# Encoder layer, attention stage: probability-value products 128 columns wide, scores over all 128 rows, the sink as a score column

## What is computed

```python
N_HEADS, N_KV_HEADS, HEAD_DIM, BLOCK = 8, 2, 64, 128        # GROUP = 4 query heads for each key/value head
scores = einsum('bnqkgd,bnskd->bnkgqs', qb, kb) * HEAD_DIM ** -0.5   # 128 queries against 3 * 128 keys
scores = scores - slopes * dist
scores = where(valid, scores, -1e30)
probs = softmax(concatenate([scores, sink_logit], -1), -1)[..., :-1]
out = einsum('bnkgqs,bnskd->bnqkgd', probs, vb)
```

## Time and profile before

| what | value |
|---|---|
| time, median of 3 runs | 3343.45 us (3343.38 to 3344.64) |
| profiled execution, its own time | 3344.08 us |
| span of the profiled execution | 3342.5 us |
| busy over the span: PE, DVE, ACT, POOL | 3062.5, 1164.3, 714.6, 487.1 us |
| mean granted clock of PE | 0.896 of full speed |
| attention part of the mixers | from about 803 us to about 1257 us of the span |

### The profile page before, as it was taken

One profiled execution on the slowest core, in us unless ns is written; L12 is line 12 of the kernel. 1 busy time (PEld: TensorE's weight loads), 2 busy tenths in 40 slices (PEclk: granted clock), 3 DMA queues, 4 the chain that ended last, 5 costly groups with the idle time before them and its releaser, 6 DMA issues. The chain is left out here.

```text
span 3342.5 us, 36601 instructions
## 1 busy us (share of the span) xinstructions
PE 3062.5 (92%) x13014; PEld 2447.1 (73%) x13014; DVE 1164.3 (35%) x1396; ACT 714.6 (21%) x1160; POOL 487.1 (15%) x829
## 2 busy tenths in 40 slices
PE   6699999838999997898894999999999997999998
PEld 5588888636666665687783788888888886788886
DVE  5000000167656550643333422222222222323432
ACT  4011111114333331500212311111111111212221
POOL 1530000164875000000111000000000000000111
PEclk9899999968555558899997999999999998999999
DMA  3322221241111005443544211111111113534553
GB/s 120 76 75 75 75 72 62 73 59 29 33 33 33 24 25 100 162 163 123 188 138 120 72 48 50 50 50 49 39 44 50 50 44 113 150 88 131 169 153 121
DMA packets 298294, 278.18 MB, mean 83 GB/s; under 512 B 46337, under 2 KB 269825, under 8 KB 288513
## 3 DMA queue, kind: packets, MB, share of 16 engines
q1 hardware_dynamic: 253536, 160.94, 17.2%
q0 software_dynamic: 13248, 68.16, 5.7%
q10 hardware_dynamic: 31456, 48.42, 4.7%
HBM read 191.50 MB, written 83.89 MB: 82 GB/s over the span
## 5 line engine op out<-in xcount | busy, mean ns | idle before, releaser
L325 PE MATMUL gu_banks<-gu_feat_hi,gu_w_hi 128*128 128x512 f32 (+1 forms) x1408 | 549.8, 391 | 1.0 <-DVE gu_feat_lo L235 1.0
L326 PE MATMUL gu_banks<-gu_feat_hi,gu_w_lo 128*128 128x512 f32 (+1 forms) x1408 | 548.4, 389 | 0.0
L327 PE MATMUL gu_banks<-gu_feat_lo,gu_w_hi 128*128 128x512 f32 (+1 forms) x1408 | 548.3, 389 | 0.0
L325 PE MATMUL pi_banks<-pi_feat_hi,pi_w_hi 128*128 128x512 f32 (+1 forms) x832 | 326.7, 393 | 31.0 <-DVE pi_w_lo L317 30.1
L327 PE MATMUL pi_banks<-pi_feat_lo,pi_w_hi 128*128 128x512 f32 (+1 forms) x832 | 324.9, 391 | 0.0
L326 PE MATMUL pi_banks<-pi_feat_hi,pi_w_lo 128*128 128x512 f32 (+1 forms) x832 | 324.9, 391 | 0.0
L325 PEld LDWEIGHTS gu_banks<-gu_feat_hi,gu_w_hi 128*128 128x128 f32 x1408 | 264.9, 188 | 55.9 <-DVE gu_feat_lo L235 1.4
L327 PEld LDWEIGHTS gu_banks<-gu_feat_lo,gu_w_hi 128*128 128x128 f32 x1408 | 264.7, 188 | 55.1
L326 PEld LDWEIGHTS gu_banks<-gu_feat_hi,gu_w_lo 128*128 128x128 f32 x1408 | 264.8, 188 | 54.7
L325 PE MATMUL dn_y<-dn_w_hi,dn_f_hi 128*128 128x512 f32 x704 | 280.0, 398 | 23.5 <-DVE dn_w_lo L802 23.5
L326 PE MATMUL dn_y<-dn_w_hi,dn_f_lo 128*128 128x512 f32 x704 | 279.5, 397 | 0.0
(11 more groups left out here) (236 smaller groups left out, 4346.1 us busy)
## 6 DMA issues: line engine op xcount, KB each, us to landing
dn_f_raw<-f SPq DMA_DIRECT2D x64, 704.0 KB, 5.9
f<-gu_conv POOLq DMA_DIRECT2D x22, 1024.0 KB, 4.1
gates<-pi_rows_out ACTq DMA_DIRECT2D x16, 1024.0 KB, 4.3
br_rows<-gates POOLq DMA_DIRECT2D x16, 1024.0 KB, 7.0
pi_w_raw<-in_w_in SPq DMA_DIRECT2D x26, 512.0 KB, 4.8
gu_w_raw<-in_w_ffn_gate SPq DMA_DIRECT2D x22, 512.0 KB, 3.8
gu_w_raw<-in_w_ffn_up SPq DMA_DIRECT2D x22, 512.0 KB, 3.8
dn_w_raw<-in_w_ffn_down POOLq DMA_DIRECT2D x22, 512.0 KB, 6.4
```

Source lines behind the costliest of these rows:

```text
L325: pe.matmul(out, w_hi, x_hi, start=first, stop=False)
L326: pe.matmul(out, w_lo, x_hi, start=False, stop=False)
L327: return pe.matmul(out, w_hi, x_lo, start=False, stop=last)
```

## The change

Five things are edited in `attention_and_scan`, and the shift tiles of four stages.

1. `weigh` multiplies the turned probabilities with the values of both key/value heads, 128 columns in place of 64. `o_psum` becomes one buffer of two banks, one for each group of four heads, and the norm reads the 64 columns that belong to the group.
2. `score` contracts over all 128 rows. The keys of both key/value heads lie in the two halves of the partitions; the queries of a head lie in their own half, and the other half is zero, set once by two memsets on DVE. The queries come in two DMAs a block instead of one.
3. The sink is column 384 (256 in the last block) of the score row: a bias column, a PSUM column that holds zero, and one more column for mask and exponential, so that the row sum already contains the sink. In the last block one small copy for each head puts it there.
4. The norm loses L1889, L1978 and L1894. What is left (the reciprocal and two multiplies of 128x256) is done at head 0 of the next block.
5. Because the output buffer is single, the first product of each group in a block waits for the norm of that group of the block before (`attn_ready`).
6. The shift tile of gu shrinks from 160 to 96 columns; those of dn (32), br (16) and ou (4) are gone. That of pi stays at 96.

```diff
-        m.sb("shift", [P, 160])
+        m.sb("shift", [P, 96])
...
-    views = carve(region, {"bias": (P, (N_HEADS, KEYS)), "q": (HEAD, (2, N_HEADS, P)), "k": (HEAD, (2, N_KV, KEYS)),
-                           "neg_scores": (P, (2, KEYS)), "probs": (P, (2, KEYS))})
+    WIDE = KEYS + 8
+    views = carve(region, {"bias": (P, (N_HEADS, WIDE)), "q": (P, (2, N_HEADS, P)), "k": (P, (2, KEYS)),
+                           "neg_scores": (P, (2, WIDE)), "probs": (P, (2, WIDE))})
...
-    o_psum = m.psum("o_psum", [P, 2, BANK])
+    o_psum = m.psum("o_psum", [P, N_KV, group, KV])
...
-            sync.dma_start(q[:, s], q_rows[:, :, bass.ds(b * P, P)]).then_inc(q_in[s], 16)
+            for g in range(N_KV):
+                sync.dma_start(q[g * HEAD:(g + 1) * HEAD, s, g * group:(g + 1) * group],
+                               q_rows[g, :, :, bass.ds(b * P, P)]).then_inc(q_in[s], 16)
...
-            pe.matmul(s_psum[:, h % 2, part], q[:, s, h, :], k[:, s, h // group, part],
+            pe.matmul(s_psum[:, h % 2, part], q[:, s, h, :], k[:, s, part],
                       start=True, stop=True).then_inc(scores_done, 1)
...
+            if h % group == 0:
+
+                pe.wait_ge(attn_ready, (i * 2 + s) * N_KV + (g + 1))
             for j in range(lo, hi):
-                pv = pe.matmul(o_psum[:, s, h * HEAD:(h + 1) * HEAD], probs_t[:, h % 2, j * P:(j + 1) * P],
-                               v[:, s, j, g * HEAD:(g + 1) * HEAD], start=j == lo, stop=j == hi - 1)
+                pv = pe.matmul(o_psum[:, g, h % group, :], probs_t[:, h % 2, j * P:(j + 1) * P],
+                               v[:, s, j, :], start=j == lo, stop=j == hi - 1)
...
+            if kind == "last":
+                dve.tensor_copy(neg_scores[:, h % 2, 2 * P:2 * P + 1], neg_sinks[:, h:h + 1]).then_inc(sink_put, 1)
...
-            dve.tensor_tensor(total[:], sums[:, s], sink_exp[:], ALU.add).then_inc(share_step, 1)
-            dve.wait_ge(share_step, b * 2 + 1)
-            dve.reciprocal(share[:], total[:]).then_inc(share_step, 1)
+            dve.reciprocal(share[:], sums[:, s]).then_inc(share_step, 1)
...
+            for g in range(N_KV):
+                mine = slice(g * group, (g + 1) * group)
+                dve.tensor_tensor(attn[:, mine], o_psum[:, g, :, g * HEAD:(g + 1) * HEAD],
+                                  share[:, mine].rearrange("p (h a) -> p h a", a=1).broadcast_to([P, group, HEAD]),
+                                  ALU.mult).then_inc(attn_ready, 1)
...
-                if kind != "first":
-                    if h == 0:
-                        open_norm(*before)
-                    if h == 2:
-                        norm(*before)
+                if kind != "first" and h == 0:
+                    norm(*before)
...
+        for g in range(N_KV):
+            dve.memset(q[g * HEAD:(g + 1) * HEAD, :, (1 - g) * group:(2 - g) * group], 0.0).then_inc(pads_zero, 1)
```

More of the change, by code:

```diff
@@ L1684, in attention_and_scan @@
     v_ready = m.sem("v_ready")
-    gap_ready = m.sem("gap_ready")
-    sink_ready = m.sem("sink_ready")
+    pads_zero = m.sem("pads_zero")
+    sink_put = m.sem("sink_put")
     share_step = m.sem("share_step")
@@ L1693, in attention_and_scan @@
         scan.add_semaphores(m)
-    q_rows = qkv[0:ATTN, :].rearrange("(h d) t -> d h t", d=HEAD)
-    k_rows = qkv[ATTN:ATTN + KV, :].rearrange("(h d) t -> d h t", d=HEAD)
+    q_rows = qkv[0:ATTN, :].rearrange("(g h d) t -> g d h t", g=N_KV, d=HEAD)
+    k_rows = qkv[ATTN:ATTN + KV, :]
     v_src = qkv[ATTN + KV:ATTN + 2 * KV, :]
@@ L1702, in keys_of, with with_sink @@
         return lo, hi, slice(lo * P, hi * P)
+    def with_sink(kind):
+        lo, hi, _ = keys_of(kind)
+        return slice(lo * P, hi * P + 1)
     def over_blocks(engine, body):
@@ L1724, in load @@
             sync.wait_ge(loaded_free, b + 1)
-            sync.dma_start(q[:, s], q_rows[:, :, bass.ds(b * P, P)]).then_inc(q_in[s], 16)
+            for g in range(N_KV):
+                sync.dma_start(q[g * HEAD:(g + 1) * HEAD, s, g * group:(g + 1) * group],
+                               q_rows[g, :, :, bass.ds(b * P, P)]).then_inc(q_in[s], 16)
             keys = bass.ds(b * P + (lo - 1) * P, (hi - lo) * P)
-            sync.dma_start(k[:, s, :, part], k_rows[:, :, keys]).then_inc(k_in[s], 16)
+            sync.dma_start(k[:, s, part], k_rows[:, keys]).then_inc(k_in[s], 16)
             sync.dma_start(v_rows[:, s, part], v_src[:, keys]).then_inc(v_in[s], 16)
@@ L1785, in weigh @@
             pe.wait_ge(probs_t_ready, i * (2 * N_HEADS) + (s * N_HEADS + h + 3))
+            g = h // group
             if h == 0:
                 pe.wait_ge(v_ready, i * 2 + s + 2)
-                pe.wait_ge(attn_ready, i * 2 + s + 1)
-            g = h // group
+            if h % group == 0:
+                pe.wait_ge(attn_ready, (i * 2 + s) * N_KV + (g + 1))
             for j in range(lo, hi):
-                pv = pe.matmul(o_psum[:, s, h * HEAD:(h + 1) * HEAD], probs_t[:, h % 2, j * P:(j + 1) * P],
-                               v[:, s, j, g * HEAD:(g + 1) * HEAD], start=j == lo, stop=j == hi - 1)
+                pv = pe.matmul(o_psum[:, g, h % group, :], probs_t[:, h % 2, j * P:(j + 1) * P],
+                               v[:, s, j, :], start=j == lo, stop=j == hi - 1)
             pv.then_inc(pv_done, 1)
@@ L1797, in turn_attn @@
             b = i * 2 + s
-            pe.wait_ge(attn_ready, b + 3)
+            pe.wait_ge(attn_ready, b * N_KV + 2 * N_KV)
             if not isinstance(b, int) or b:
@@ L1838, in _ @@
         pe.wait_ge(warmed, 1)
+        pe.wait_ge(pads_zero, N_KV)
         turn_values(0, 0, "first")
@@ L1848, in mask @@
         def mask(i, s, kind, h):
-            part = keys_of(kind)[2]
+            part = with_sink(kind) if kind != "last" else keys_of(kind)[2]
             n = i * (2 * N_HEADS) + (s * N_HEADS + h)
             dve.wait_ge(exp_done, n + 1)
+            if kind == "last":
+                dve.tensor_copy(neg_scores[:, h % 2, 2 * P:2 * P + 1], neg_sinks[:, h:h + 1]).then_inc(sink_put, 1)
             dve.wait_ge(scores_done, n + 1)
@@ L1884, in copy_values @@
             dve.tensor_copy(v[:, s, lo:hi].rearrange("p a b -> p (a b)"), v_psum[:, part]).then_inc(v_ready, 1)
-        def open_norm(i, s):
-            dve.wait_ge(masked, (i * 2 + s) * N_HEADS + (N_HEADS + 2))
-            dve.tensor_tensor(sink_gap[:], sinks[:], neg_top[:, s], ALU.add).then_inc(gap_ready, 1)
         def norm(i, s):
             b = i * 2 + s
-            dve.wait_ge(sink_ready, b + 1)
-            dve.tensor_tensor(total[:], sums[:, s], sink_exp[:], ALU.add).then_inc(share_step, 1)
-            dve.wait_ge(share_step, b * 2 + 1)
-            dve.reciprocal(share[:], total[:]).then_inc(share_step, 1)
-            dve.wait_ge(share_step, b * 2 + 2)
+            dve.wait_ge(exp_done, b * N_HEADS + (N_HEADS + 2))
+            dve.reciprocal(share[:], sums[:, s]).then_inc(share_step, 1)
+            dve.wait_ge(share_step, b + 1)
             dve.wait_ge(pv_done, b * N_HEADS + (N_HEADS + 2))
@@ L1930, in _ @@
             slope = 2.0 ** (-8.0 * (h + 1) / N_HEADS)
-            dve.tensor_scalar(bias[:, h, :], distance_f[:], -slope * HEAD ** 0.5, None, ALU.mult)\
+            dve.tensor_scalar(bias[:, h, 0:KEYS], distance_f[:], -slope * HEAD ** 0.5, None, ALU.mult)\
                 .then_inc(bias_step, 1)
@@ L1934, in _ @@
         dve.tensor_scalar(neg_sinks[:], sinks[:], -1.0, None, ALU.mult).then_inc(bias_step, 1)
-        dve.wait_ge(bias_step, 3 + N_HEADS)
+        dve.tensor_scalar(bias[:, :, KEYS], sinks[:], HEAD ** 0.5, None, ALU.mult).then_inc(bias_step, 1)
+        dve.memset(s_psum[:, :, KEYS:KEYS + 1], 0.0).then_inc(bias_step, 1)
+        dve.wait_ge(bias_step, 5 + N_HEADS)
         dve.sem_inc(masked, 2)
@@ L1938, in _ @@
         dve.sem_inc(v_ready, 1)
-        dve.sem_inc(attn_ready, 2)
+        dve.sem_inc(attn_ready, N_KV)
         copy_values(0, 0, "first")
@@ L1959, in exponentials @@
         def exponentials(i, s, kind, h):
-            part = keys_of(kind)[2]
+            part = with_sink(kind)
             n = i * (2 * N_HEADS) + (s * N_HEADS + h)
             act.wait_ge(masked, n + 3)
+            if kind == "last":
+                act.wait_ge(sink_put, h + 1)
             act.wait_ge(turned, n + 1)
@@ L1997, in attend @@
                 copy_turned(i, s, kind, h)
[L1998 to L2002, removed]
+                if kind != "first" and h == 5:
+                    copy_out(*before)
         act.sem_inc(exp_done, 2)
@@ L2009, in _ @@
         over_blocks(act, attend)
-        sink_part(TILES // 2 - 1, 1)
         copy_out(TILES // 2 - 1, 1)
```

15 lines of the change are left out of this document (1 added, 14 removed).

## The result

| | before | after |
|---|---|---|
| median, us | 3343.41 (4 runs, 3341.70 to 3344.64) | 3159.76 (4 runs, 3158.07 to 3161.46) |
| profiled execution, its own time, us | 3344.08 | 3158.07 |
| span, us; mean granted clock | 3342.5; 0.896 | 3156.5; 0.959 |

The ratio is 0.9451, with a 95% interval from 0.9435 to 0.9467: 5.5% faster. The forecast was 3202 us with a range from 3170 to 3245. The time lies 42 us under the forecast and 10 us under the range.

The account below looks back on a forecast made before the run. PE at 1.2 GHz was taken to bound the attention; at full clock its parts sum to 302 us, a 145 us gain, less 4 for clock drops. 3344.1 - 141 - 0.6 = 3202 us, range 3170 to 3245.

Parts of the forecast that it names:

- the hole around the score: PE time lost entering and leaving the 64-row score matmul in attention; 0.38 us a head taken as saved, bounds 0 and 0.38.
- Rivals 2 and 3: Attention clock stays 1.2 GHz: only 0.38 us a head won, 3298 us (0.08); or products pay width, 3376 us (0.03).
- rival 1: In the attention, the clock rises and falls again whenever DVE holds PE up; 3235 us, chance 0.14.
- Pads. ... I take 0: Shift tile edits in gate_up, down, out and branches, priced at no gain or loss.
- The bound of -12 us for down: Down's 2112 matmuls at 0.2264 us, gate_up's pace; the low end of -12 to +12 us.
- Phases 1 to 5: Five stretches of attention at full clock, priced mostly from DVE's work: 106, 26, 39, 86 and 30 us.
- phases 1, 2, start: Blocks 0 to 7: start 1 us, 46 heads beside POOL's large steps 106 us, 14 beside small steps 26 us.
- phase 3: Blocks 8 and 9: 6 heads at 2.2 us beside POOL's small steps, 10 at 2.6 awaiting its large ones; 39 us.
- phases 4, 5: Blocks 10 to 14: 27 heads at 3.2 us beside POOL, 86 us; then 13 at 2.3 us without it, 30 us.
- Phase 1: Blocks 0 to 7 beside POOL's large steps: DVE needs 18.4 us for eight heads; 46 heads, 106 us.
- Small parts: Attention's memsets and start 1 us on the path; extra query DMA hidden; new norm wait taken as 0.
- the clock allowance: 4 us taken off the attention's gain for stretches where DVE is so late that the clock drops for a while.

Follow-up runs that it names:

- narrow_products: Changed kernel with products back at 64 columns of the values, scores still over 128 rows; 3162.85 us.
- rows_64: Changed kernel with scores again over the 64 rows of the head's own half, products still 128 columns wide; 3184.72 us.
- narrow_rows_64: Changed kernel with both taken back, products 64 columns wide and scores over 64 rows; 3324.50 us.

## Why the prediction was right and wrong

**Direction and mechanism: right.** The clock rose and stayed at 1.00 (0.93 in blocks 12 to 14), the hole around the score is closed (the score takes 0.75 us at full clock, and 3.58 us a head is back when both edits are undone), product width costs next to nothing, and DVE beside POOL then sets the time. Rivals 2 and 3 did not happen. Of rival 1 there is a trace in the clock of 0.93. In such a block DVE is busy for 23.48 of 24.00 us anyway, so the 4 us taken off for it were probably too much; no run prices them.

The reason given for the rise, that with rows and width mended the stream has no hole, is supported and not complete. With both undone the clock stays at 0.50. But `narrow_products` keeps the clock up with its narrow products, and `rows_64` reaches 1.00 with the hole at each score, and then falls and stays low for up to 20.5 us. So the rows count for more than the width, which the prediction did not tell apart.

**"Pads. ... I take 0": the first step that failed, by 20 us.** It is about half of the miss. The bound of -12 us for down was worked out from gate_up's pace in the earlier trace rows, and it is what happened; out gave more than the 3 us allowed for both small stages (6.3 with 2.3 in branches). What failed is the reason for taking 0, that the pads are small and the moves multiples of 64 bytes. All the pad settings say that a distance of 0 modulo 256 is the fast one, and that 32, 64 and 128 bytes off cost nearly the same, 2.5 to 3%. The same rows held the answer: gate_up, at 0.2264, had the operands at a distance of 0 before and after, and down, at 0.2322, had 128 and went to 0.

**Phases 1 to 5: the second step that failed, 18 us too long.** From forecast to measured, each stretch up to the start of the next one's first mask on DVE:

| stretch | forecast, us | measured, us |
|---|---|---|
| up to the end of block 7 (phases 1, 2, start) | 133 | 123.2 |
| blocks 8 and 9 (phase 3) | 39 | 30.6 |
| blocks 10 to 14 (phases 4, 5) | 116 | 113.9 |
| last block and tail | 14 | 16.3 |

*Phase 1* was priced from one stretch of 20.05 us, the eight heads of the earlier trace rows. It held two of the dearest scan steps (their five parts 7.11 and 6.75 us; over 825 to 930 us of the kernel before the mean is 6.22). After the change the five means make 6.11 us, of which the groups above show three, and a block is 17.1 us, not 18.4. Two steps a block make that 1.6 us less, a little more than the difference.

*Phase 3* was taken as DVE work beside POOL, 2.2 and 2.6 us a head. The windows of blocks 8 and 9 show PE busy for all of their 14.39 and 14.13 us: PE's floor was the bound, 1.80 and 1.77 us a head. (The table has 2 us more, as it goes by DVE's masks, whose lead over PE changes at the ends of this phase.)

*Phases 4 and 5* came out right as a sum, and wrong inside. 3.2 us a head was forecast beside POOL up to 1067 us and 2.3 behind; measured were 2.4 to 3.0 all the way, because POOL ended its scan only at 1080.5 us and phase 5 never came. Its fifteen steps of that phase began at 959.9 us, not 955, and took 8.0 us each, not 7.5:

```profile
1079.49 1.03 POOL L2072 TENSOR_TENSOR sm_states<-sm_states,sm_by_im 128x240 f32 x1
```

**Small parts: held.** The memsets take 0.91 us each and the first mask begins 0.6 us later (804.33 for 803.70); 1 us was forecast. So small a shift can't be told from chance: in the runs made from the changed kernel the first turn of values lies between 801.3 and 805.3 us. The new wait at the first product of a block, taken as 0, ends ten waits of PE of 2.6 us in all (0.36 us at 854.90 in the timeline above).

**The whole.** Of the 42 us, 20 are pads, 18 the phases and 4 the clock allowance. The range left the result out, and would have done so with its own low bounds taken together: 15 us of pads and 10% of phases 1 and 4, 19 us, lead to 3168 us. Phase 3, the pads beyond their bound and the clock allowance were in none of them.

**Slips in the working.** The first three move the forecast by less than 1 us. The 0.38 us a head are 0.29 in the score, 0.06 in the transpositions and 0.03 in the products. Fifteen POOL steps of 8.3 us from 795 us end at 919.5, not 916. The phases add up to 1111.3 us, not 1111.5. The factor 1.49 sets 512 columns against 480; at the same size it is about 1.4, which would have made phase 4 some 4 us shorter. It was luck that this did no harm: after the change the five parts of that phase took 1.52 times as long as free of POOL (6.19 us for 4.06).

## What to carry to other kernels

- When PE is busy for the whole of a window and the granted clock reads 0.50, the busy share says nothing about how near it is to its best: look for what breaks the stream, such as one matmul with fewer rows than its neighbours or narrow ones. Mending the rows was enough here. Mending the width alone brought the clock up late and lost it again three times, and still won 140 of the 165 us.
- Price a phase from the group means over the phase, not from its first steps; and for the phase that a faster engine opens up, write down the floor of every engine before taking one as the bound.
- Where two stages do the same work at different paces and only the operands' addresses differ, take the faster pace as the price of the address, and look at both operands' distance in the built program, with the allocator's rounding.

## What the runs showed of the hardware

- The clock can stay at 0.50 through blocks in which PE never pauses (30.10 of 30.10 us in `narrow_rows_64`), while blocks with pauses of PE run at 1.00 (16.41 of 17.10 us after the change).
- Once it has fallen behind waits of PE, how long it stays low differs with the stream: 13.7 and twice 20.5 us in `rows_64`, with scores over 64 rows, and under 4 us each time between 1005 and 1080 us of the changed kernel, with 128 rows.
- A float32r matmul stream is 2.5 to 3% slower (0.2324 to 0.2333 us for 0.2267) when the distance of its two operands in a partition is 32, 64 or 128 bytes modulo 256 than when it is 0, and 1% slower at 192 (0.2289); in this kernel that is 48 us between the best and the worst setting tried.
- POOL at work beside DVE lengthens DVE's 128x512 operations from 1.04 to between 1.33 and 1.69 us, and a 128x8 operation from 0.16 to as much as 1.23 us; such an operation ends 0.02 to 0.03 us behind POOL's.
